# Expert weight planes of a mixture-of-experts layer: two transfers of 4 KB runs in place of one of 8 KB runs

## The reference

```python
xb = xf[tok]
hid = jax.nn.silu(jnp.einsum('nrd,ndf->nrf', xb, wg[e].astype(F32))) * jnp.einsum('nrd,ndf->nrf', xb, wu[e].astype(F32))
yb = jnp.einsum('nrf,nfd->nrd', hid, wd[e].astype(F32)) * w[..., None]
acc = acc.at[tok.reshape(-1)].add(yb.reshape(-1, D_MODEL))
```

## Time and profile before

| | |
|---|---|
| median of 3 runs | 2057.23 us (2054.04 to 2058.53) |
| the profiled execution | 2054.86 us, its span 2053.1 us |
| TensorE busy | 1992.9 us, 97% of the span |
| VectorE, GpSimd, ScalarE busy | 1134.7, 781.3, 505.2 us |
| DMA | 370.45 MB in 129639 packets, of which q1 314.83 MB and q0 54.61 MB |
| mean granted TensorE clock | 0.993 of full speed |

### The profile page before, as it was taken

The page is one execution under the profiler, slowest core; times in us unless marked ns, Lnnn a source line. Parts: engine busy times, 40 slices in busy tenths (PEclk is TensorE's granted clock), DMA queues, the critical chain, the costliest instruction groups (busy, mean ns, idle before and its releaser), DMA issues.

```text
span 2053.1 us, 23779 instructions
## 1 busy us (share of the span) xinstructions
PE 1992.9 (97%) x7241; PEld 1005.4 (49%) x7242; DVE 1134.7 (55%) x3064; ACT 505.2 (25%) x1103; POOL 781.3 (38%) x717
## 2 busy tenths in 40 slices
PE   8999999999999999999999999999999999999994
PEld 6444667575544444444445554444444444444441
DVE  6221546776622222344776757966666666666645
ACT  3111554452312222224331221111111111111114
POOL 1762005622122221215990002654555545454531
PEclk9999999999999999999999999999999999999997
DMA  5421000011132222135257014999999999999964
GB/s 148 125 96 41 21 21 21 22 47 47 41 129 77 77 82 75 49 114 175 96 201 285 31 42 151 361 362 361 354 363 355 369 350 355 350 341 355 339 216 172
DMA packets 129639, 370.45 MB, mean 180 GB/s; under 512 B 33712, under 2 KB 65668, under 8 KB 103832
## 3 DMA queue, kind: packets, MB, share of 16 engines
q1 hardware_dynamic: 103960, 314.83, 41.3%
q0 software_dynamic: 23520, 54.61, 10.5%
q10 hardware_dynamic: 2080, 0.01, 0.1%
HBM read 320.57 MB, written 68.17 MB: 189 GB/s over the span
## 4 chain that ended last, share of the span: by engine, by line
PE 25%; DMA 20%; issue 4%; POOL 3%; DVE 3%; POOLq 0%; ACT 0%; SPq 0%; DVEq 0%
DMA sums<-arena,row_to 19%; PE banks L3219 9%; PE banks L2300 4%; PE banks L3235 4%; PE banks L2347 2%; POOL arena L2136 2%; PE banks L2014 2%; PE banks L279 1%; PE banks L2364 1%; PE banks L2323 1%; DVE arena L3212 1%; DVE index L3182 1%; DMA arena<-in_w_router_dram 0%; DVE arena L3337 0%; PE banks L3227 0%
## 5 line engine op out<-in xcount | busy, mean ns | idle before, releaser
L3219 PE MATMUL banks<-arena 128*128 128x512 f32 x1056 | 467.7, 596 | 3.9 <-issue 3.2
L3198 POOL DMA_INDIRECT arena<-h_rows,index x268 | 282.5, 1054 | 133.4 <-issue 78.8
L3219 PEld LDWEIGHTS banks<-arena 128*128 128x128 f32 x1056 | 197.4, 192 | 228.4 <-issue 228.4
L1720 PE MATMUL banks<-arena 128*128 128x512 f32 x672 | 299.0, 594 | 1.0 <-ACT arena L323 1.0
L3235 PE MATMUL banks<-arena 128*128 128x512 f32 x528 | 237.6, 593 | 1.3 <-ACT arena L3033 0.8
L3206 POOL DMA_INDIRECT sums<-arena,row_to x66 | 109.0, 1652 | 268.4 <-DMA sums<-arena,row_to 229.0
L279 PE MATMUL banks<-arena 128*128 128x512 f32 x416 | 192.1, 599 | 2.2 <-PEq L108 2.2
L1720 PEld LDWEIGHTS banks<-arena 128*128 128x128 f32 x672 | 123.1, 190 | 135.5 <-issue 133.9
L3212 DVE STREAM_TRANSPOSE arena<-arena 128x1024 f32<-128x1024 f32 x66 | 133.7, 2026 | 57.6 <-PE banks L3219 57.5
L3182 DVE TENSOR_SCALAR index<-row 32x1 uint32<-32x1 f32 x1072 | 155.2, 145 | 17.1
L3235 PEld LDWEIGHTS banks<-arena 128*128 128x128 f32 x528 | 100.1, 190 | 126.5 <-issue 124.8
(11 more groups left out here) (414 smaller groups left out, 2424.0 us busy)
## 6 DMA issues: line engine op xcount, KB each, us to landing
arena<-in_w_exp_gate_dram SPq DMA_DIRECT2D x66, 1024.0 KB, 7.1
arena<-in_w_exp_up_dram SPq DMA_DIRECT2D x66, 1024.0 KB, 10.6
arena<-in_w_exp_down_dram SPq DMA_DIRECT2D x66, 1024.0 KB, 16.4
arena<-in_w_in_dram SPq DMA_DIRECT2D x26, 1024.0 KB, 5.3
gates<-arena SPq DMA_DIRECT2D x60, 256.0 KB, 2.0
arena<-gates SPq DMA_DIRECT2D x15, 1024.0 KB, 7.6
arena<-h_rows,index POOLq DMA_INDIRECT x268
arena<-in_x_dram SPq DMA_DIRECT2D x8, 512.0 KB, 5.8
```

What stands on the lines that cost most here:

```text
L1720: mm = pe.matmul(gate_bank(n, b), left[:, k, :], right[:, k, :], start=(alone and k == 0), stop=(k == 3), skip_group_check=True)
L3198: return pool.indirect_dma_start(w.x[k][:, 256 * q:256 * (q + 1)], None, rows, bass.IndirectOffsetOnAxis(ap=g.index[:, k, q:q + 1], axis=0 ...
L3219: mm = pe.matmul(g.bank[:, 2, :].rearrange("p (a f) -> p a f", a=2), xT[:, k, :], wgu[:, :, k, :], start=(k == 0), stop=(k == KT - 1))
```

## The change

Each plane is asked for as two transfers, the first with floats 0 to 1023 of every partition and the second with floats 1024 to 2047: 128 runs of 4 KB each, 512 KB a transfer, where it was 128 runs of 8 KB and 1 MB. The destinations, the bytes and the moments at which SyncE asks are the same. The semaphore values for which TensorE waits are doubled.

```diff
-    sp.dma_start(g.region(at, 2048), expert_plane(g, e, "w_exp_gate")).then_inc(done, 16)
-    sp.dma_start(g.region(at + 2048, 2048), expert_plane(g, e, "w_exp_up")).then_inc(done, 16)
+    for i, name in enumerate(("w_exp_gate", "w_exp_up")):
+        for h in range(2):
+            sp.dma_start(g.region(at + 2048 * i + D * h, D),
+                         expert_plane(g, e, name)[:, D * h:D * (h + 1)]).then_inc(done, 16)
...
-    sp.dma_start(g.region(RING[slot] + 4096, 2048),
-                 expert_plane(g, e, "w_exp_down")).then_inc(done or g.exp_down_in[slot], 16)
+    for h in range(2):
+        sp.dma_start(g.region(RING[slot] + 4096 + D * h, D),
+                     expert_plane(g, e, "w_exp_down")[:, D * h:D * (h + 1)]).then_inc(done or g.exp_down_in[slot], 16)
...
-                pe.wait_ge(g.exp_in[c % 4], (quarter(i, c) + 1) * 32)
+                pe.wait_ge(g.exp_in[c % 4], (quarter(i, c) + 1) * 64)
...
-                pe.wait_ge(g.exp_down_in[c % 4], (quarter(i, c) + 1) * 16)
+                pe.wait_ge(g.exp_down_in[c % 4], (quarter(i, c) + 1) * 32)
...
-                pe.wait_ge(loaded, (o + 1) * 48)
+                pe.wait_ge(loaded, (o + 1) * 96)
```

## The result

The change made the kernel slightly slower. Over 5 runs it took 2066.61 us (2063.03 to 2067.81), against 2057.97 us (2054.04 to 2059.93) for 5 runs of the kernel before: a ratio of 1.0039, 95% interval 1.0024 to 1.0054, some 8 us. The forecast was 2045.

What follows compares the result with a forecast made beforehand. From about 1534 us the scatter chain was taken to bound the kernel, TensorE before. Scatters -11.4, late weights +0.8, last weights +0.9, last scatter -2.1 gave -11.8: 2054.86 to 2043.1 profiled, 2045 forecast as median, range 2040 to 2061.

Steps and rivals of the forecast that it cites:

- SyncE, three more issues at 0.33 us, hidden: SyncE's queue: some 1.0 us more issuing per expert, covered by its 9 us wait for free ring slots; cost nothing.
- The scatter chain leaves the path, -11.4: Expert stage: shorter runs bring scatter steps from 11.24 us to under TensorE's 10.83, saving 11.4 us.
- The weights' own rate, +0.27 per expert: Weight transfers: 407 instead of 422 GB/s, so an expert's three planes take 7.73 us instead of 7.46.
- Supply of 10.92 before and 11.19 after; the reserve lasts 40 experts: Weights' queue: us per expert against TensorE's 10.83, 0.36 late each; 14.3 us reserve, then TensorE falls 5.0 us late.
- The exit absorbs 4.2: Loop's exit, turn 59 to 60: TensorE stands 4.2 us anyway, so weights 5.0 late cost only 0.8.
- The last weights +0.9: End of the stage: the last weights cost perhaps 0.9 us more.
- the last scatter -2.1: End of the stage: without the scatters' lag the last scatter goes off about 2.1 us earlier.
- The sum: Whole kernel: -11.4 + 0.8 + 0.9 - 2.1 = -11.8 us.
- the weights become the bound and take more than is won: TensorE's wait on gate and up planes: supply of 11.41 to 11.5 us per expert, 2058 to 2061 us; chance 0.17.
- More room: Weight supply: quicker scatters waste less engine time, TensorE alone sets the pace, 2043.7 us or a little under; chance 0.10.
- Exposed transfers: Weight transfers: fixed 1.5 us each without overlap, 4.5 us per expert, 270 over 60, about 2325 us; chance 0.01.

Runs made afterwards that it cites:

- e10: The change run again, unaltered, against the kernel before: 2063.21 us, ratio 1.0038.
- e11: Repeat run of the kernel before with three transfers per expert as there, each in two runs of 4 KB a partition: 2062.72 us, ratio 1.0022.
- e5: Kernel before, with SyncE asking for a block's gate and up planes only when the previous block's have landed: 2059.95 us, ratio 1.0008.
- e13: The change, with the rows of odd expert blocks placed from partition 127 downwards: 2040.03 us, ratio 0.9914 to the kernel before.
- e16: The change, with every block's rows dealt out evenly over the partitions: 2040.68 us, ratio 0.9915 to the kernel before.
- e15: Kernel before (8 KB runs), with every block's rows dealt out evenly over the partitions: 2040.11 us, ratio 0.9910.
- e12: Kernel before (8 KB runs), with the rows of odd expert blocks placed from partition 127 downwards: 2042.06 us, ratio 0.9920.
- e4: Kernel before, with three transfers per expert as there, each in two runs of 4 KB a partition: 2062.20 us, ratio 1.0027.
- e9: Kernel before, with three transfers per expert as there, each in four runs of 2 KB a partition: 2078.86 us, ratio 1.0103.
- e8: Kernel before, with only the up plane halved into two transfers of 4 KB runs: 2060.02 us, ratio 1.0011.
- e14: Kernel before (8 KB runs), with the rows of all expert blocks placed from partition 127 downwards: 2065.08 us, ratio 1.0039.
- e3: Kernel before, with each plane cut by partitions into two transfers of 64, runs still 8 KB: 2342.62 us, ratio 1.1395.
- e6: The change, with down planes of odd blocks left out after the first four, a sixth of expert bytes: 2041.35 us, ratio 0.9915 to the kernel before.
- e7: Kernel before (8 KB runs), with down planes of odd blocks left out after the first four, a sixth of expert bytes: 2040.98 us, ratio 0.9916.
- e2: Kernel before, with only gate and up planes halved into two transfers of 4 KB runs each: 2066.88 us, ratio 1.0049.

## Why the prediction was wrong

- **SyncE, three more issues at 0.33 us, hidden.** The size was wrong: issues of gate and up planes take 1.0 to 1.4 us at the median and up to 6.7, presumably since the queue is full. The conclusion, cost nothing, held within the few us that e10 against e11 leave open (also e5, e13, e16).
- **The scatter chain leaves the path, -11.4.** Right. In the first 26 steps scatters went 11.24 us apart; now (1634.1 - 1345.6) / 26 = 11.10, which is TensorE's own pace there, and no wait of ScalarE or VectorE for them is left. e16 against e15 shows the same effect without other troubles.
- **The weights' own rate, +0.27 per expert.** Right as a rate (409 against 422 GB/s). From turn 33 to 59 a block's time rose by less, from 11.27 to 11.28 (e10) and 11.38 us (the profile above).
- **Supply of 10.92 before and 11.19 after; the reserve lasts 40 experts.** This is the step that failed. It lasted 12 (13 in e10): turn 17 is the last on time. From there a block was 0.54 us late and not 0.36, and by turn 59 TensorE was 607.8 - 54 x 10.83 = 23.0 us late instead of 5.0. Supply was worked out from the bytes of the whole queue, a mean over everything that moves them, whereas a block waits until the slowest part of its plane has landed. In the scatters the lower places carry more rows than the mean, and there the path must already have been over its limit: with even places the same bytes keep up with TensorE in both forms (e12 and e15, e13 and e16), so the mean load alone makes no plane late.
- **Where it was hidden.** Before, scatters went every 11.24 us while TensorE turned every 10.83: in 26 steps they fell 11 us behind, and this postponed work let the weights arrive on time until turn 33. The shorter runs let scatters keep pace, and the weights give way instead, from turn 17 on. Thus 8.6 us of the loss lie in blocks 17 to 33, and only 3.0 after them, where both kernels are held by the same full path. This reading is argued from the paces; the runs show the limit and its removal, not who passes whom.
- **The exit absorbs 4.2.** The exit got 2.3 us shorter, for another reason. It takes 12.3 us where nothing is late (e12, 1927.8 to 1940.1) and also where the weights are late (e4, e9), and 13.6 to 15.0 only where ScalarE waits for scatters up to it (before, e5, e8, e14). So TensorE's own 1.5 over its pace is all that can absorb late weights, and most of the 2.3 belongs to the scatters. **The last weights +0.9, the last scatter -2.1:** together -0.1.
- **The sum**, with the measured terms: -11.4 + 23.0 - 2.3 - 0.1 = +9.2, instead of -11.8.
- **The rivals.** What happened is the rival "the weights become the bound and take more than is won", at its place, before the up products, and beyond its upper end (2061). It had a chance of 0.17. Its supply of 11.41 was close to the 11.37 (turns 17 to 33) and 11.38 (33 to 59) measured, but it started from the same long reserve. "More room" described the kernels with even places: TensorE alone, 2040 us. "Exposed transfers", priced at 270 us, is excluded by e10 and e11. The rule of the Trainium skill on 1 MiB per DMA ("DMA: Bandwidth & Descriptors", "Rules for kernel authors") decides little in this queue: six transfers of 512 KB took 2063.21 us and three of 1 MB 2062.72. The 2.0 us per DMA of "Anatomy of one DMA" in the same page of the Trainium skill are stated there for GpSimd's transfers, and the weights are SyncE's.

The page of the Trainium skill that bears on the cause was not used in the prediction. "SBUF — State Buffer", section "Door 1: The DMA port swizzle (why `[64,N]` ≈ `[32,N]`)", says that partitions 0 to 63 are reached by only 8 of 16 ports, and 64 to 127 by the other 8. The trace agrees: halves of 64 partitions moved 217 GB/s (e3), whole planes 422. By that rule a scatter of 96 rows placed from 0 upwards loads one half of the ports with 64 rows and the other with 32. Whether the overfull part here is a port or a DMA engine no run tells apart.

## What to carry to other kernels

When DMA is full, work out the load of its fullest part and not the mean: a transfer that skips rows should skip them evenly over the partitions, and here a table of places that does it costs one constant. Take a reserve computed from mean bytes as an upper bound, since a tile is there only when its slowest part is. And a busy share of 1.0 is compatible with lost rate: here 351 and 368 GB/s both read as full.

## What was unexpected of the hardware

- Cutting a 128-partition transfer into two halves of 64 halved the rate (217 against 422 GB/s) with the DMA share at 1.01.
- An issue on SyncE's queue, 0.33 us in the kernel before, took 5.44 us in the row above and up to 6.7 us, with no wait shown: it appears as SyncE's own work in the chain.
- A run of 4 KB a partition moved at 409 to 412 GB/s, one of 8 KB at 421 to 424, and e9's 2 KB at 388, all beside nothing indirect.
- With all weights loaded and even places, a scatter beside 4 KB runs hardly keeps the next one waiting (11.6 us in all, e16), beside 8 KB runs nearly always (181.9 us, e15). The length of the companion's runs is not all: with a sixth of the bytes left out it is 126.7 us beside 4 KB (e6) and 93.5 beside 8 KB (e7), and with gate and up halved still 194.4 (e2). That was not settled.
